# A gated delta rule whose chunk inverse starts from 32 by 32 blocks, with its decay rows spread by two wide fp32r products

## The reference

```python
def chunked_gated_delta_rule(q, k, v, beta, g):
    beta, gc = c3(beta), jnp.cumsum(c3(g), axis=-1)
    decay = jnp.exp(jnp.where(incl, gc[..., :, None] - gc[..., None, :], -jnp.inf))
    kb = k * beta[..., None]
    lower = jnp.where(strict, jnp.einsum('bhnid,bhnjd->bhnij', kb, k) * decay, 0.0)
    tmat = jnp.eye(CHUNK, dtype=jnp.float32) + lower
    u = lax.linalg.triangular_solve(tmat, v * beta[..., None], left_side=True,
                                    lower=True, unit_diagonal=True)
    w = lax.linalg.triangular_solve(tmat, kb * jnp.exp(gc)[..., None], left_side=True,
                                    lower=True, unit_diagonal=True)
    ...
```

## Time and profile before

| | |
|---|---|
| median of 3 timed runs | 1060.01 us (1059.55 to 1061.75) |
| profiled execution: span | 1056.6 us |
| median less span (what lies around the span) | 3.4 us |
| PE busy | 1025.6 us, 97% |
| PEld busy | 886.4 us, 84% |
| POOL / DVE / ACT busy | 712.2 / 599.0 / 577.4 us |
| mean granted clock of TensorE | 0.997 |

### The profile page before, as it was taken

How to read it: one execution, slowest core, us unless ns; L and a number is a source line. 1 busy time by engine, 2 the same in 40 slices (tenths; PEclk the granted TensorE clock), 3 DMA queues, 4 the chain that set the end, 5 groups by cost and what they waited for, 6 DMA issues and landing times.

```text
span 1056.6 us, 18561 instructions
## 1 busy us (share of the span) xinstructions
PE 1025.6 (97%) x7112; PEld 886.4 (84%) x7112; DVE 599.0 (57%) x1181; ACT 577.4 (55%) x968; POOL 712.2 (67%) x550
## 2 busy tenths in 40 slices
PE   8999999999999999999999998999999989999986
PEld 8988998888877988899888887788888768888875
DVE  4774366786565557246584563517446560646564
ACT  4754347656644574336656744445576534567652
POOL 4786537872648787556766645897366978744794
PEclk9999999999999999999999999999999999999999
DMA  8664434653425555435444332665233546423451
GB/s 294 192 179 122 139 101 131 173 156 107 134 100 153 180 165 157 140 84 157 141 139 141 115 125 87 209 191 158 81 113 120 186 140 216 133 91 108 140 183 57
DMA packets 80584, 151.59 MB, mean 143 GB/s; under 512 B 6448, under 2 KB 12400, under 8 KB 80496
## 3 DMA queue, kind: packets, MB, share of 16 engines
q1 hardware_dynamic: 80496, 150.41, 46.9%
HBM read 149.34 MB, written 1.05 MB: 142 GB/s over the span
## 4 chain that ended last, share of the span: by engine, by line
PE 88%; DVE 4%; ACT 3%; POOL 3%; issue 2%; DMA 0%; POOLq 0%; SPq 0%; DVEq 0%; ACTq 0%
PE bulk L941 53%; PE bulk L926 12%; PE chain L962 5%; PE chain L970 4%; PE chain L1039 4%; PE chain L1307 1%; PE bulk L934 1%; PE chain L1288 1%; ACT arena L1347 1%; PE chain L1163 1%; PE chain L1179 1%; POOL w_lo L868 1%; DVE arena L1846 1%; PE chain L1030 1%; POOL w_lo L866 1%
## 5 line engine op out<-in xcount | busy, mean ns | idle before, releaser
L866 POOL TENSOR_TENSOR w_lo<-raw,w_hi 128x512 fp32r<-128x512 f32 (+3 forms) x259 | 340.7, 1316 | 292.4 <-ACT w_hi L1347 291.8
L868 POOL TENSOR_TENSOR w_lo<-raw,w_hi 128x512 fp32r<-128x512 f32 (+3 forms) x277 | 375.6, 1357 | 31.8 <-ACT w_hi L1347 31.8
L1347 ACT ACTIVATE w_hi<-raw 128x1024 fp32r<-128x1024 f32 (+4 forms) x277 | 277.3, 1019 | 210.1 <-PE bulk L941 163.4
L941 PE MATMUL bulk<-w_hi,hT_hi 128*128 128x512 f32 (+1 forms) x756 | 306.0, 405 | 0.8 <-ACT arena L1347 0.5
L941 PE MATMUL bulk<-w_hi,hT_lo 128*128 128x512 f32 (+1 forms) x756 | 294.4, 389 | 0.0
L941 PE MATMUL bulk<-w_lo,hT_hi 128*128 128x512 f32 (+1 forms) x756 | 204.2, 389 | 1.9 <-POOL w_lo L868 1.9
L941 PEld LDWEIGHTS bulk<-w_hi,hT_hi 128*128 128x128 f32 x756 | 142.4, 188 | 33.5 <-issue 1.9
L941 PEld LDWEIGHTS bulk<-w_lo,hT_hi 128*128 128x128 f32 x756 | 141.7, 188 | 32.7 <-POOL w_lo L868 3.4
L941 PEld LDWEIGHTS bulk<-w_hi,hT_lo 128*128 128x128 f32 x756 | 142.5, 188 | 26.8 <-issue 1.0
L926 PE MATMUL bulk<-hT_hi,w_hi 128*128 128x256 f32 x384 | 96.3, 289 | 0.0
L926 PE MATMUL bulk<-hT_lo,w_hi 128*128 128x256 f32 x384 | 94.0, 282 | 0.0
(11 more groups left out here) (262 smaller groups left out, 1393.4 us busy)
## 6 DMA issues: line engine op xcount, KB each, us to landing
raw<-in_w_in_dram SPq DMA_DIRECT2D x194, 512.0 KB, 3.6
raw<-in_w_out_dram SPq DMA_DIRECT2D x32, 512.0 KB, 3.7
raw<-in_w_branch_dram SPq DMA_DIRECT2D x16, 512.0 KB, 3.7
raw<-in_w_mem_kv_dram SPq DMA_DIRECT2D x8, 512.0 KB, 3.4
raw<-in_w_merge_up_dram SPq DMA_DIRECT2D x16, 256.0 KB, 2.9
raw<-in_w_in_dram SPq DMA_DIRECT2D x8, 420.0 KB, 3.4
gain<-in_ln_rows_dram SPq DMA_DIRECT2D x4, 512.0 KB, 5.3
gain<-in_gains_dram SPq DMA_DIRECT2D x3, 512.0 KB, 6.1
```

The lines of the kernel that those rows point to most:

```text
L866: pool.tensor_tensor(lo_of(p, u)[:, 0:at], raw_of(p, u)[:, 0:at], hi_of(p, u)[:, 0:at].bitcast(F32), ALU.subtract).then_inc(first_part, 1)
L868: pool.tensor_tensor(lo_of(p, u)[:, at:n], raw_of(p, u)[:, at:n], hi_of(p, u)[:, at:n].bitcast(F32), ALU.subtract).then_inc(p.done("split" ...
L941: m = pe.matmul(dst, a, part[:, k, :], start=(first and not low and k == 0 and i == 0), stop=(last and low and k == nk - 1))
L1347: return act.activation(dst, src, func, **more)
```

## The change

**Inverse.** `x1` and the levels 0 and 1 are done on the four 32 by 32 diagonal blocks by a new `quad_blocks`, with 32 products for a call. X, its transpose and Y are then 32 columns wide for each of the eight matrices. After level 0 ACT copies X and its transpose into the layout of 64 columns with masks (new step `x2`, four instructions), and DVE subtracts the results of level 1 into that layout with two instructions each (`apart`). Level 2 and 3 stay as they were. `sub` ends with one instruction instead of eight.

**Rows.** `rn` writes the decays and the strengths twice each, 104 columns in all. ACT writes them to `row_parts` in fp32r, with a sign; two new instructions of DVE (`avT`) make of that a high and a low part, and `row_heads`, 104 rows by four blocks of 128 columns. `dec` is then two products of 512 columns in fp32r, whose weights are a column of `pick`.

**Constants and order.** The table of constants has 1377 columns instead of 1841 (some are now read as broadcasts). `ORDER` is new as a whole; the steps are the same but for the four `x2`.

```diff
@@ def shape_constants():
+    for n, sign in enumerate((1, 1, -1, -1)):
+        c[:, K_PART + n] = sign * (p[:, 0] // QUAD % 2 == n % 2)
...
@@ def gdn_chain(g):
+        if n == 0:
+            out.append(("x2", g))
@@ ORDER = (
-    "aaaaasammssvamsmssaamaaasaacsccasscccssammcmmsmaacssmmaacssccsmmmamaaasasmdabsmaaabssmmcsmaammassdbm"
+    "aaaaasavssssmmaamasammassaaacccsmcssamaccscammamscsmaamcmsmaccmasssaasamsmdsabaammssbammaammsabdmssa"
...
+                def quad_blocks(c, pair, col=0):
+
+                    for j in range(R * 4):
+                        for at in quads:
+                            a, b = pair(j, at)
+                            m = pe.matmul(c[at, col + j * QUAD:col + (j + 1) * QUAD], a, b, start=(j == 0), stop=(j == R * 4 - 1),
+                                          skip_group_check=True)
+                    return m
...
                 def dec(g, r):
                     c = take("dec", g, r)
-                    pe.wait_ge(*p.after("scalar", "avT", g))
-                    for j in range(4):
-                        pe.matmul(c[:, j * P:(j + 1) * P], spread(4 * r + j, 8), rows_T[0:8, :],
-                                  start=(j == 0), stop=(j == 3), skip_group_check=True)
-                        m = pe.matmul(c[:, 512 + j * P:512 + (j + 1) * P], spread(4 * r + j, 8, 64), rows_T[64:72, :],
-                                      start=(j == 0), stop=(j == 3), skip_group_check=True)
+                    pe.wait_ge(*p.after("vector", "avT", g))
+                    rows = row_heads[0:ROWS, :, :].rearrange("p j n -> p (j n)")
+                    for n in range(2):
+                        m = pe.matmul(c[:, n * 512:(n + 1) * 512], pick[0:ROWS, 2 * n + r:2 * n + r + 1].broadcast_to([ROWS, P]),
+                                      rows, start=True, stop=True)
...
@@ PE, def invZ(g, n):
+                    if n < 2:
+                        quad_blocks(c, lambda j, at: (xtq[at, j, :], yq[at, j, :]))
+                        quad_blocks(c, lambda j, at: (yq[at, j, :], xtq[at, j, :]), 512).then_inc(p.done("invZ"), 1)
...
+@@ ACT
+                def x2(g):
+
+                    act.wait_ge(*p.after("vector", "invX", g, 0))
+                    for to, of in ((xh, xq), (xth, xtq)):
+                        for n in range(2):
+                            ins = A(to[:, :, n * QUAD:(n + 1) * QUAD], of, ACT.Copy, scale=cst[:, K_PART + n:K_PART + n + 1])
+                    ins.then_inc(p.done("x2"), 1)
...
+@@ DVE
+                def avT_(g):
+
+                    v.wait_ge(*p.after("scalar", "avT", g))
+                    c = half("avT", g)[0:ROWS, :]
...
+                    STT(c[:, P:2 * P], c[:, 0:P], cst[0:ROWS, K_LOW:K_LOW + 1], row_parts[0:ROWS, :].bitcast(F32),
+                        ALU.mult, ALU.add).then_inc(p.own, 1)
+                    v.wait_ge(*p.last())
+                    TT(row_heads[0:ROWS, :, :], over(c[:, P:2 * P], 4), bc(cst[0:ROWS, K_HEAD:K_HEAD + 4], P), ALU.mult).then_inc(
+                        p.done("avT"), 1)
...
+                def apart(to, c):
+
+                    for k in range(2):
+                        x = to[:, :, k * QUAD:(k + 1) * QUAD]
+                        ins = STT(x, c, cst[:, K_PART + 2 + k:K_PART + 3 + k], x, ALU.mult, ALU.add)
+                    return ins
```

More of the change, by code:

```diff
@@ L1497, in avT_ @@
                     act.wait_ge(*p.after("tensor", "avT", g))
-                    A(rows_T[0:72, :], half("avT", g)[0:72, 0:P], ACT.Copy).then_inc(p.done("avT"), 1)
+                    A(row_parts[0:ROWS, :], half("avT", g)[0:ROWS, 0:P], ACT.Copy, scale=cst[0:ROWS, K_SIGN:K_SIGN + 1]).then_inc(
+                        p.done("avT"), 1)
                 def stat(w, g):
@@ L1993, in invY @@
                     v.wait_ge(*p.after("tensor", "invY", g, n))
+                    if n < 2:
+                        at, w = level_mask(n)
+                        TT(yq, heads(half("invY", g, n)[:, 0:R * 4 * w], R * 4), over(cst[:, at:at + w], R * 4),
+                           ALU.mult).then_inc(p.done("invY"), 1)
+                        v.wait_ge(*p.here("invY"))
+                        return None
                     c, up = heads(half("invY", g, n)[:, 0:R * 4 * HALF], R * 4), halves[1]
@@ L1997, in invY @@
                     else:
-                        m = cst[:, K_LEVEL + n * HALF:K_LEVEL + (n + 1) * HALF]
-                        TT(yh, c, over(m, R * 4), ALU.mult).then_inc(p.done("invY"), 1)
+                        at, w = level_mask(n)
+                        TT(yh, c, over(cst[:, at:at + w], R * 4), ALU.mult).then_inc(p.done("invY"), 1)
                     v.wait_ge(*p.here("invY"))
+                def apart(to, c):
[3 more added lines that the diff above has]
+                    return ins
                 def invZ(g, n):
                     v.wait_ge(*p.after("tensor", "invZ", g, n))
+                    if n < 2:
+                        c = heads(half("invZ", g, n)[:, 0:R * 4 * QUAD], R * 4)
+                        if n == 0:
+                            TT(xq, xq, c, ALU.subtract).then_inc(p.done("invZ"), 1)
+                        else:
+                            v.wait_ge(*p.after("scalar", "x2", g))
+                            apart(xh, c).then_inc(p.done("invZ"), 1)
+                        v.wait_ge(*p.here("invZ"))
+                        return None
                     c, (low, up) = heads(half("invZ", g, n)[:, 0:R * 4 * HALF], R * 4), halves
@@ L2012, in invX @@
                 def invX(g, n):
+                    if n < 2:
+                        c = heads(half("invZ", g, n)[:, 512:512 + R * 4 * QUAD], R * 4)
+                        if n == 0:
+                            TT(xtq, xtq, c, ALU.subtract).then_inc(p.done("invX"), 1)
+                        else:
+                            apart(xth, c).then_inc(p.done("invX"), 1)
+                        v.wait_ge(*p.here("invX"))
+                        return None
                     c = heads(half("invZ", g, n)[:, 512:512 + R * 4 * HALF], R * 4)
@@ L2424, in handlers @@
                             norm_c=norm_c, hT=hT, drain_v=drain, gmul=gmul, tap=tap, tap_on=tap_on, ba_a=ba_a, ba_c=ba_c, gc=gc_, stat=stat, rn=rn,
-                            dec=dec, dec_c=dec_c, kk=kk, rep=rep, sub=sub, kT=kT, vT=vT, invY=invY, invZ=invZ, invX=invX, kq=kq, ks=ks, o=o_,
+                            avT=avT_, dec=dec, dec_c=dec_c, kk=kk, rep=rep, sub=sub, kT=kT, vT=vT, invY=invY, invZ=invZ, invX=invX, kq=kq, ks=ks, o=o_,
                             onorm_a=onorm_a, onorm_c=onorm, zgain=zgain, kinorm_a=kinorm_a, rope_i=rope_i, raw=raw_, topk=topk,
```

103 lines of the change are left out of this document (63 added, 40 removed).

## The result

| | before | after |
|---|---|---|
| median of 4 timed runs | 1060.88 us | 1052.61 us (1049.79 to 1053.04) |
| ratio, 95% interval | | 0.9917 (0.9894 to 0.9941) |
| profiled execution: span | 1056.6 us | 1048.0 us |
| mean granted clock of TensorE | 0.997 | 0.995 |

The kernel became faster by 0.8%, or 8.8 us by the ratio; 21 had been forecast, and the time lies inside the stated range but at less than half of the forecast gain. The profiled execution is 8.6 us shorter than that of before, so it can be taken apart. Every timed run is 1.7 to 1.9 us longer than its own span: the 3.4 us in the table of before hold 1.6 by which its profiled execution was shorter than the median one, and the profiled execution of the changed kernel, 1049.79 us, is the shortest of its four.

The account below looks back on a forecast made before the run. PE, busy 1025.6 of 1056.6 us, bounds the kernel. 1056.6 − 5.8 − 11.9 − 6.3 + 3 = 1035.6 us of span, 3.4 more for the timed median: 1039; own range 1033 to 1046, 8 in 10 1033 to 1056.

Parts of the forecast that it names:

- `dec`, −5.8: Eight `dec` calls on PE: two fp32r records, 0.46 us instead of 1.18, gain 0.72 each, 5.8 us.
- 32 by 32 blocks, −11.9: 28 calls in `x1`, `invY`, `invZ`: four records side by side in 32 ns, 0.425 us less each, −11.9 us.
- The rival with records one after another: PE takes block records singly at 29.4 ns: blocks term +26.3 us, kernel 1077; chance 0.13.
- the page's rule: Successive matmuls start at least about 25 ns apart: group of four at least 100 ns, term +18.5, kernel near 1069.
- terms 1 and 2: Eight `dec` calls, −5.8 us, and 28 calls with 32 by 32 blocks, −11.9 us.
- Waits, −6.3, and +3 allowed for new ones: `gT` 1 −2.7, `mT` 1 −1.9, half clock behind it −1.7 us; +3 for unfound waits of the new order.
- the three moves: `o0` unit ahead of `gT` 1; `split` and `gmul` out of the way ahead of `mT` 1: −6.3 us together.
- The cover, costed at nothing: Units on PE hide DVE's `avT` and ACT's four copies for each group; 11.7 us if all cover were gone.
- the second rival: Only two of four block records run side by side: 64 ns a group, +2.3 us, kernel near 1053; chance 0.15.
- The third rival: Waits stay, or longer ways to `dec` and `invZ` 1 make new ones: 1048, at worst 1054; chance 0.10.
- the two signs of being wrong: A call of 64 records over 1.1 us, or new PE waits for `avT`, `x2` or the levels over 5 us.
- term 3's marks: In the profile: `gT` 1 without a wait, `mT` 1 with about 1 us, no stretch at 0.50 behind it.

Follow-up runs that it names:

- the third term alone: Kernel before with second unit of `o0` ahead of `gT` 1, `split` behind `onorm`, `gmul` behind `onorm_a`: 1.0000 (0.9985 to 1.0015).
- the shifted start: Changed kernel with 8 filler products fewer at its start (12 instead of 20); ran once, time not compared.
- the units between: Changed kernel with two units moved in layer 1, group 0, between `invY` and `invZ` 0 and 1: 0.9883, 1046.64 us.
- the endings: Changed kernel with a `split` behind `gT` 0, `gmul` behind `mT` 0, second unit of `o1` ahead of `mT` 1: 0.9921 (0.9897 to 0.9945).

## Why the prediction was wrong in size

The direction held, the gain was less than half. Step by step:

- **`dec`, −5.8.** Right: 0.47 us for a call, so 0.71 less each.
- **32 by 32 blocks, −11.9.** Right in mechanism and nearly in size: 33 ns for a group and 0.39 to 0.40 us for a call, −11.1. The rival with records one after another would have needed 117 ns, the one with two pairs 64. Four records in 33 ns also settle the page's rule that was weighed there, that of the Trainium skill, TensorE: Matmul & The Clock Gate, section "Wait — 56ns, not 53.3ns?": 25 ns is no floor for products in different rows and columns of the array.
- **What no term had: +3.0.** The calls became so short that PE twice used up its instructions. The prediction counted twice as many records and asked only how fast PE takes them, not how fast they arrive. The prediction named one place with nothing but transposes between two calls; in layer 1, where the stops came, `invY` 1 and `invZ` 1 are another. With units between the calls the stops are gone, and the gain of the new instructions against the old in the same order is then 1.0054 − 0.9883 = 0.0171, 18 us, as terms 1 and 2 said (17.7); the intervals leave 3 to 4 us either way.
- **Waits, −6.3, and +3 allowed for new ones.** This is the step that failed: term 3. The order alone costs 5.7 us where it was to gain 3.3. Taken alone the three moves gave nothing: the one at `gT` 1 ran into POOL, which the earlier trace rows show busy for 6.30 of 6.30 us right there, and the one at `mT` 1 put POOL's work beside DVE's. The prediction read both waits as lateness of one chain and didn't ask what the next engine in line was doing. Its 1.9 us at `mT` 1 were too many in any case: the table load could not begin near 634.9, since DVE's queue came to `gmul`, and so to the small instruction behind it, only at 635.21; in the experiment it began at 635.49. And that a wait of one microsecond would leave the clock alone was wrong, too: behind 1.27 us it fell at another place.
- **The cover, costed at nothing.** Right for the new order: no wait of the changed kernel names `avT` or `x2`. In the old order it would have been wrong by nearly the whole gain. So the new order isn't an addition to the gain, as the sum had it; it is what the gain needs, at a price of its own.
- **Rivals and signs.** The measured 1052.6 lies next to the second rival's 1053, but that is luck, since four records take 33 ns and not 64. The third rival, with 0.10, had the mechanism in part: the waits did not go, and new ones came, though not through `avT` or `x2`. Its 1054 should be 1057, unless the +3 is left out; and the bounds given for the forecast's own range make 1035 to 1052 and not 1033 to 1046. Neither of the two signs of being wrong appeared, since both looked at the new instructions and none at the order; and two of term 3's marks came, `gT` 1 without a wait and 1.1 us at `mT` 1, though the term gave nothing.

The sum, with what was measured: −5.7 and −11.1 for the instructions, +3.0 for the stops, +5.7 for the order, −8.1; the ratio says −8.8. This takes the order to cost the new instructions what it costs the old. The changed kernel's own trace comes close: 6.0 us more at waits, 3.0 of them the two stops, and some 2 that are left over in delays too short for the list, so about 5 for the order.

What stays open: why single instructions of DVE stretch to 5 to 9 us in some profiles. POOL's splits ran one after another beside them, which would fit the shared ports, but no run here took POOL's work away. Six of the eight profiles of kernels in the new order have such a row (not that of the changed kernel), and one of the six in the old order, that of the third term alone; the difference was not tested further.

## What to carry to other kernels

A gain in instructions and the order that carries it are to be priced together: try the new instructions in the old order, and the old ones in the new, before adding the two. Before a wait is booked as a gain, look at which engine is next in line there; if it is busy without a pause, or if the moved work slows it, the wait only changes its name. Where products are split into many small ones, count the instructions per microsecond as well as the time of one.

## What the runs showed of the hardware

Four fp32 products of 32 by 32 on the four diagonal blocks of the array run side by side, 33 ns for four records where two of 64 by 64 took 58.8. PE can run out of instructions: twelve stops inside calls of `quad_blocks`, in seven kernels, all came at the same remainder of 193 of 256 records (matmuls, weight loads and semaphores), 0.4 to 2.4 us long. The Trainium skill, Runtime: NRT & Kernel Launch, section "Instruction fetch mechanics", says that instructions come in blocks of 16 KB, 256 of them, and that the cost is mostly hidden. The traces agree on the blocks; at 33 ns for eight instructions the cost is not hidden. A wait of 1.27 us of PE was followed by 3.40 us at half clock at one place, one of 2.72 us at another by none, so the length of a wait alone doesn't tell. The wait of 1.27 us is in five profiles: in the four with the new instructions (the changed kernel, the shifted start, the units between, the endings) the clock fell behind it, with the old instructions in the new order it stayed at 1.00; in the three kernels without that wait it did not fall there. What decides stays open.
